# Two layers of a diffusion backbone with expert retrieval on one core: query/key norms moved beside the last projection chunks, and new item weights

## The reference, cut to what matters

```python
for l in range(2):                                   # two layers
  for group in (prompt: 128 tokens, samples: 256 tokens):
    h = rms_norm(x, norm1_g[l]) * (1 + sc1) + sh1
    qa, ka, va, qb, kb, vb, ci, cb, cc = split(h @ w_in[l])        # 1024 -> 2560 columns
    qa, ka, qb, kb = rms_norm per head, times a gain               # all "query/key norms"
    if samples: qa, ka, qb, kb = rotate (2-D axial) ; keys, values += cached 128 tokens
    oa = softmax(qa ka^T / 8) va                                   # 6 heads (group A)
    ob = (softmax(q1 k1^T) - lam * softmax(q2 k2^T)) vb            # 6 heads, two maps each (group B)
    oc = cb * conv3(cc * ci)                                       # short convolution
    x = x + g1 * (norms(oa, ob, oc) @ w_out[l])
    h = rms_norm(x, norm2_g[l]) * (1 + sc2) + sh2
    scores = (h @ wq[l]) . sub_keys        # 8 retrieval heads, two halves of 128 keys
    16 best experts per token and head; gate = softmax of their scores
    x = x + g2 * sum_k gate_k * gelu(u_tab[e_k] . h) * v_tab[e_k]
```

## Time and profile before

| | us |
|---|---|
| median of 3 runs | 3009.83 |
| the runs | 2999.77, 3009.83, 3010.87 |
| the profiled execution | 3009.86, its span 3008.1 |
| PE / DVE / ACT / POOL busy | 1561.5 / 1619.3 / 282.0 / 1557.0 |
| moved from HBM | 959 MB, 320 GB/s over the span; 805 MB of it by the gathers |

### The profile page before, as it was taken

The page is one execution under the profiler, slowest core; times in us unless marked ns, Lnnn a source line. Parts: engine busy times, 40 slices in busy tenths (PEclk is TensorE's granted clock), DMA queues, the critical chain, the costliest instruction groups (busy, mean ns, idle before and its releaser), DMA issues.

```text
span 3008.1 us, 21921 instructions
## 1 busy us (share of the span) xinstructions
PE 1561.5 (52%) x6476; PEld 687.7 (23%) x6476; DVE 1619.3 (54%) x3970; ACT 282.0 (9%) x734; POOL 1557.0 (52%) x1601
## 2 busy tenths in 40 slices
PE   6665757857334443335345584775733334233345
PEld 2334325525201110111123132543510000000001
DVE  1414686653664756454741288655376575766510
ACT  0211003211000000010000001311100000000000
POOL 0002531256667666535565664125667767776665
PEclk8777865678656776657677796578866665656556
DMA  8677992379999999858998986248989999999988
GB/s 283 248 249 255 367 342 71 102 287 386 386 395 401 371 384 405 310 188 326 349 397 336 408 311 246 63 143 313 371 341 387 403 382 391 393 394 381 376 331 336
DMA packets 299015, 963.25 MB, mean 320 GB/s; under 512 B 28280, under 2 KB 30712, under 8 KB 298128
## 3 DMA queue, kind: packets, MB, share of 16 engines
q0 software_dynamic: 221184, 805.40, 70.2%
q1 hardware_dynamic: 77712, 156.44, 14.3%
HBM read 959.12 MB, written 2.62 MB: 320 GB/s over the span
## 4 chain that ended last, share of the span: by engine, by line
DMA 25%; PE 24%; DVE 20%; POOL 15%; issue 14%; ACT 1%; SPq 0%; POOLq 0%; DVEq 0%; ACTq 0%
DMA ring<-peer_v,v_rows 15%; POOL ring L659 14%; DVE ring L1453 9%; PE ps_acc L920 7%; DMA ring<-peer_u,u_rows 6%; PE ps_mm L743 3%; PE ps_mm L797 3%; PE ps_mm L858 2%; PE ps_mm L886 2%; PE ps_mb L823 1%; DMA weights<-w_in 1%; DMA weights<-peer_wq 1%; PE ps_tr L808 1%; DMA weights<-ada_w 1%; PE ps_mb L682 1%
## 5 line engine op out<-in xcount | busy, mean ns | idle before, releaser
L920 PE MATMUL ps_acc<-ring,coef_cols 128*32 128x512 f32 x3072 | 619.3, 948 | 1119.1 <-DMA ring<-peer_v,v_rows 1119.0
L659 POOL DMA_INDIRECT ring<-peer_u,u_rows x768 | 784.8, 1022 | 686.3 <-DVE dots L1453 469.3
L659 POOL DMA_INDIRECT ring<-peer_v,v_rows x768 | 748.6, 975 | 423.0 <-issue 230.7
L1453 DVE CUSTOM_DVE_ANT_0 ring<-ring,ps_tr 128x1024 f32<-128x1024 f32 x512 | 618.0, 1220 | 369.0 <-DMA ring<-peer_u,u_rows 352.1
L920 PEld LDWEIGHTS ps_acc<-ring,coef_cols 128*32 128x32 f32 x3072 | 123.2, 146 | 1539.6 <-issue 1529.0
L1453 DVE CUSTOM_DVE_ANT_0 ring<-ring,h 128x1024 f32<-128x1024 f32 x256 | 307.7, 1223 | 112.1 <-DMA ring<-peer_u,u_rows 98.1
L743 PE MATMUL ps_mm<-weights,hT 128*128 128x512 f32 x480 | 218.8, 615 | 27.0 <-DMA weights<-w_in 22.5
L886 PE MATMUL ps_mm<-hT,weights 128*128 128x128 f32 (+1 forms) x1024 | 201.3, 356 | 21.3 <-DMA weights<-peer_wq 21.3
L886 PEld LDWEIGHTS ps_mm<-hT,weights 128*128 128x128 f32 x1024 | 172.7, 214 | 86.0 <-issue 47.4
L624 POOL TENSOR_SCALAR u_rows<-picks 128x16 uint32<-128x16 f32 x48 | 16.9, 352 | 289.1 <-DVE picks L1426 288.0
L1477 DVE TENSOR_TENSOR h<-h,ps_acc 128x1024 f32<-128x1024 f32 x6 | 7.3, 1221 | 240.9 <-PE ps_acc L920 240.9
(11 more groups left out here) (206 smaller groups left out, 1562.5 us busy)
## 6 DMA issues: line engine op xcount, KB each, us to landing
weights<-ada_w SPq DMA_DIRECT2D x24, 2048.0 KB, 10.2
weights<-w_in SPq DMA_DIRECT2D x20, 2048.0 KB, 14.5
weights<-peer_wq SPq DMA_DIRECT2D x16, 2048.0 KB, 14.3
weights<-w_out SPq DMA_DIRECT2D x8, 2048.0 KB, 14.1
ring<-peer_u,u_rows POOLq DMA_INDIRECT x768, 6.3
ring<-peer_v,v_rows POOLq DMA_INDIRECT x768, 7.0
weights<-peer_keys SPq DMA_DIRECT2D x4, 1024.0 KB, 7.1
par<-params SPq DMA_DIRECT2D x2, 1026.0 KB, 8.0
```

Source lines behind the costliest of these rows:

```text
L659: pool.indirect_dma_start(ring[:, place % RING, :], None, src, bass.IndirectOffsetOnAxis(ap=rows, axis=0)).then_inc(row_full[place % RING] ...
L920: last = pe.matmul(ps_acc[QROWS * k:QROWS * (k + 1), b * NB:(b + 1) * NB], coef_cols[:, i // PART % 2, at:at + QROWS], ring[:, slot("v", n ...
L1453: dve.tensor_tensor_reduce(row, row, h, 1.0, 0.0, ALU.mult, ALU.add, dots[:, n // UNIT % 2, n % UNIT:n % UNIT + 1]).then_inc(u_used, 1)
```

## The change

Two things are altered in `Beside` and `dense_stages`; no instruction is added or taken away.

1. The steps of the query/key norms no longer stand behind the projection. Each of the steps of chunks 3 and 4 (`late_proj`) is followed by two `qk` steps. Chunks 0 to 2 hold all query and key columns, so DVE starts when chunk 2 has been copied. ACT's square root then stands between two copies of the projection.
2. A step yields its kind, and the weight comes from one table for the samples and the first prompt (`False` is not the prompt) and another for the prompt.

```diff
-W_NORM, W_PROJ, W_QK, W_KEYS_T, W_HEAD, W_TILE, W_OUT, W_PQ = 4, 20, 2, 2, 2, 4, 16, 5
+QK_CHUNKS = 3
+WEIGHTS = {False: dict(norm=4, proj=20, late_proj=8, qk=2, keys_t=2, tile=4, head=4, out=18, pq=8),
+           True: dict(norm=10, proj=9, late_proj=9, qk=3, keys_t=3, tile=8, head=7, out=9, pq=5)}
+def steps(tiles):
+    nt = len(tiles)
+    kinds = ["norm"] * nt
+    for i in range(IN_CHUNKS * nt):
+        kinds += ["late_proj", "qk", "qk"] if i >= QK_CHUNKS * nt else ["proj"]
+    kinds += ["keys_t"] * (1 if tiles == P_TILES else 3)
+    kinds += (["tile"] + ["head"] * HEADS + ["tile"]) * nt
+    return kinds + ["out"] * (OUT_CHUNKS * nt) + ["norm"] * nt + ["qk"] + ["pq"] * 16
 def dense_weight(tiles):
+    return sum(WEIGHTS[tiles == P_TILES][kind] for kind in steps(tiles))
...
         while self.done < self.due - 1e-6 and self.done < self.weight:
-            self.done += next(self.program)
+            self.done += self.weights[next(self.program)]
...
 # PE
                         last.then_inc(proj_mm, 1)
-                        yield W_PROJ
-                for j in range(QK_PARTS * nt):
-                    yield W_QK
+                        yield "late_proj" if n >= QK_CHUNKS else "proj"
+                        if n >= QK_CHUNKS:
+                            yield from ("qk", "qk")
...
 # DVE
+                def qk_parts():
+                    dve.wait_ge(proj_ready, nth(l, tiles, IN_CHUNKS, QK_CHUNKS * nt - 1))
...
+                parts = qk_parts()
                 for i in range(IN_CHUNKS * nt):
-                    yield W_PROJ
-                dve.wait_ge(proj_ready, nth(l, tiles, IN_CHUNKS, IN_CHUNKS * nt - 1))
...
+                    yield "late_proj" if i >= QK_CHUNKS * nt else "proj"
+                    if i >= QK_CHUNKS * nt:
+                        for _ in range(2):
+                            yield next(parts)
```

More of the change, by code:

```diff
@@ L189, in chunks @@
         for tiles in (P_TILES, S_TILES):
-            nt, nk = len(tiles), 1 if tiles == P_TILES else 3
-            out = nt * (1 + IN_CHUNKS + QK_PARTS + 2 + HEADS) + nk
-            found = [(nt + n * nt, 0, [("in", l, tiles, n)]) for n in range(IN_CHUNKS)]
+            nt, kinds = len(tiles), steps(tiles)
+            proj = [at for at, kind in enumerate(kinds) if kind in ("proj", "late_proj")]
+            out = kinds.index("out")
+            found = [(proj[n * nt], 0, [("in", l, tiles, n)]) for n in range(IN_CHUNKS)]
             found += [(out + n * nt, 0, [("out", l, tiles, n)]) for n in range(OUT_CHUNKS)]
@@ L1284, in dense_stages @@
+                parts = qk_parts()
+                for i in range(IN_CHUNKS * nt):
+                    yield "late_proj" if i >= QK_CHUNKS * nt else "proj"
+                    if i >= QK_CHUNKS * nt:
+                        for _ in range(2):
+                            yield next(parts)
+                assert next(parts, None) is None
                 for j in range(nk):
-                    yield W_KEYS_T
+                    yield "keys_t"
                 for j, t in enumerate(tiles):
```

185 lines of the change are left out of this document (93 added, 92 removed).

## The result

| kernel | runs | median us | lowest to highest |
|---|---|---|---|
| before | 4 | 3010.35 | 2999.77 to 3012.99 |
| after | 4 | 3038.14 | 3034.44 to 3040.89 |

The ratio is 1.0104, with a 95% interval of 1.0088 to 1.0121: the change makes the kernel 1.0% slower. The forecast was 3051 us, slower. The profiled execution of after took 3039.41 us with a span of 3037.6 us, 29.5 us more than before.

The account below looks back on a forecast made before the run. It took full DMA engines as the bound where the stream runs undisturbed, and the ring's return trip at dense steps. Layer 0's prompt, S0, S1 and P1 summed as 3009.86 + 0 + 11 + 15 + 15 = 3051 us, range 2980 to 3085.

Parts of the forecast that it names:

- the return trip through the ring: From a DVE dot through POOL's gathers, landing and PE's quad to DVE's scores: 13.4 us, paid by dense steps behind quads.
- the walk: Step-by-step timing, with constants from the earlier trace, of the samples' output steps and of P1's heads.
- The samples' norms in S1: S1 up to the last norm step: ten dots fewer ahead of it on DVE, -12 us.
- The heads: Samples, last norm step to second tile's merge: more dots on DVE there, +10 us (S0) and +11 us (S1).
- S0's -15: S0 up to the last norm step: ten gathers of 0.52 MB fewer on full DMA engines, -15 us.
- The output steps: Samples, second merge to the dot of item 93: output projection and norm 2 wait behind quads, +17 us each.
- Items 93 to 127: Samples behind norm 2: same items and chunks in both kernels from item 94 on, so 0 us.
- P1's +15: P1's heads each wait for their own return trip, 19 us a head on average: +15 us, bounds -9 and +32.
- A: Rival, chance 0.16: gathers fill the gaps beside dense stretches, P1 gives -46 us and the kernel takes 2937 us.
- B: Rival, chance 0.22: nothing measurable; P1 0, or the samples' last two quads don't wait: 3020 us, at the lowest 3010.
- C: Rival, chance 0.08: slower still; PE bounds the samples' denser pq steps, 7 us for each group, 3082 us.
- D: Rival, chance 0.04: norms don't overlap projection, as PE waits behind ACT's square root; -15 and -12 vanish, 3078 us.

Follow-up runs that it names:

- e12: Kernel after with S0's modulation chunks at steps 5, 11, 12, 13, 17, 18, 19, none between two uses of a projection chunk: 1.0053 of before.
- e10: Kernel after with LAG 12, S0's modulation chunks moved partly to keys and heads, samples' output steps at items 75 to 82, norm 2 at 84 and 85: 0.9614 of before.

## Why the prediction was right, point by point

**Right.** The direction, and that the return trip through the ring is what decides: the item numbers were changed so that more dense steps stand alone behind a quad, and each pays the trip. In P1 the walk held step by step. Shifted by the 25.6 us that P1 starts later, the steps at items 79, 85, 90, 95, 101, 106 and 111 were due at 1244, 1269, 1286, 1304, 1332, 1351 and 1368; their scores came at 1246.2, 1270.7, 1289.6, 1305.2, 1331.9, 1351.0 and 1366.6. The samples' norms in S1 gained 16.9 us for a forecast of 12. The heads cost 3.0 and 5.6, at the lower end of their bounds (+3, all in PE's shade): PE was the bound of group B, as the earlier trace rows said, and DVE's second dot fitted in.

**S0's -15 failed as a term.** The step was that the DMA engines set S0's stretch, so that ten gathers fewer give 14.6 us. The bytes did fall, from 50.9 MB (356 GB/s over 142.9 us) to 45.6 (313 over 145.7), but the time rose by 2.8 us. I counted gathers and took the modulation chunks as three adds on DVE; their loads, and that two of them now fall between the uses of a projection chunk, were left out. The queue of SP was part of the step that moved. With the chunks elsewhere (e12) the 14.4 us are there.

**The output steps were right in kind and too small.** Forecast 110 us to the dot of item 93, measured 118.5 and 115.6. The walk had the second, third and fourth steps at +34, +55 and +85, they came at +26, +47 and +80; what was missed is behind them. There the first norm 2 waits 17.98 us for its own quad, and the norms end at +117, not +109: 36 us behind the fourth step instead of 24.

**Items 93 to 127 were not neutral.** I wrote that from item 94 on both kernels do the same. They do the same dense steps, but not the same gathers: while DVE waited, POOL had filled all 14 slots. In the 95.4 us of after 59 gathers are under way and in the 103.3 us of before 66, one of which began ahead of it. Six or seven gathers of 0.52 MB at 376 GB/s are 8.4 to 9.8 us; 7.9 (S0) and 9.8 (S1) were measured. So part of a wait inside the stream is given back, by an estimate up to the ring's content; e10 shows it from the other side.

**P1's +15 was +5.8.** From the head at item 79 to that at 111 the walk was exact to 4 us. Then it charged a return trip to the steps at items 116 and 122, but the step of the last head reads no new scores. Timeline of DVE, that step's first instruction (no wait), the merge's end and the dot of item 127:

```profile
1377.04 0.16 DVE L1326 RECIPROCAL rinv<-rowsum 128x2 f32<-128x2 f32 x1
...
1409.58 0.62 DVE L1384 SCALAR_TENSOR_TENSOR merged<-merged,par 128x384 f32<-128x384 f32 x1
...
1423.75 1.21 DVE L1479 CUSTOM_DVE_ANT_0 ring<-ring,ps_tr 128x1024 f32<-128x1024 f32 x1
```

The merge ends 14 us earlier than the walk said (1398 + 25.6 = 1424), about one trip. Between the two DVE still waits 9.37 us for ACT's exponentials of the gates and 6.27 us for the last values. From the dot of item 127 to unit 6 the two kernels differ by 1.9 us; I did not take that apart.

**The rivals.** A needed a head's cycle under 14 us, and it was 20 (six heads in 120.4 us, 1246.2 to 1366.6; the walk's own times give 20.7 where its text says 19): the argument against A was right for LAG 8. With LAG 12 P1's heads come close to what A describes: their scores come 13 to 20 us apart, beside a DMA share of 0.95. The Trainium skill's "Perfetto Trace Analysis", section "Optimization Strategy", says that interleaving such regimes may improve performance; in the kernel after it did not (1.0% slower), and whether it does with LAG 12 the runs leave open (0.994). B came half true in P1 (+5.8, between its 0 and the forecast's 15), but not in the samples' output steps, whose last two quads did wait. Its sums do not follow from its own terms either: without those waits the samples give 0 and +4, not +5 and +5, so B is 3014 and its lower figure 2999. C did not occur: items 93 to 127 became shorter. D was true of S0 in its effect (+2.8), but not for its reason: ACT's square root is in S1 as well, where the gain came.
